# A small fp32 product behind the first round of each feed-forward loop of a decoder step

## The reference

```python
x = x + 0.5 * swiglu(rms_norm(x, p['norm_ffn1']), p['ffn1_w_gu'], p['ffn1_w_down'])
h = rms_norm(x, p['norm_mix'])
z = h @ p['w_in']
...                                   # retention, RWKV-7 recurrence
merged = (jax.nn.sigmoid(zgr) * (o_ret @ p['w_ret_o'])
          + jax.nn.sigmoid(zgw) * (o_rwkv @ p['w_rwkv_o']))
x = x + merged @ p['w_out']
x = x + 0.5 * swiglu(rms_norm(x, p['norm_ffn2']), p['ffn2_w_gu'], p['ffn2_w_down'])

def swiglu(x, w_gu, w_down):
    gate, up = jnp.split(x @ w_gu, 2, axis=-1)
    return (jax.nn.silu(gate) * up) @ w_down
```

## Time and profile before

| | |
|---|---|
| three runs | 2836.80, 2853.76, 2853.82 us |
| their median | 2853.76 us |
| profiled execution | 2833.03 us, span 2831.2 us, mean granted clock 0.997 |
| PE busy | 2803.7 us (99%), 24,662 matmul records |
| DVE busy | 1563.9 us (55%) |
| ACT busy | 1116.5 us (39%) |
| matmuls of the down loops | 3 lines x 1408 |

### The profile page before, as it was taken

How to read it: one execution, slowest core, us unless ns; L and a number is a source line. 1 busy time by engine, 2 the same in 40 slices (tenths; PEclk the granted TensorE clock), 3 DMA queues, 4 the chain that set the end, 5 groups by cost and what they waited for, 6 DMA issues and landing times.

```text
span 2831.2 us, 57289 instructions
## 1 busy us (share of the span) xinstructions
PE 2803.7 (99%) x24662; PEld 2731.8 (96%) x24662; DVE 1563.9 (55%) x1679; ACT 1116.5 (39%) x1121; POOL 107.1 (4%) x144
## 2 busy tenths in 40 slices
PE   9999999999999999999999999999999999999998
PEld 8999999999999999898998999999999999999998
DVE  6544444454566576775865655466544544444454
ACT  5333333333344453544534644233433333333333
POOL 0000000000000002011020010000000000000000
PEclk9999999999999999999999999999999999999999
DMA  5444454444556543635436544555444445444454
GB/s 209 168 169 162 165 179 171 173 168 157 172 189 235 199 174 123 235 135 201 163 134 240 188 145 164 190 201 202 164 165 176 159 164 180 170 174 164 159 173 146
DMA packets 85460, 495.80 MB, mean 175 GB/s; under 512 B 10320, under 2 KB 10496, under 8 KB 44096
## 3 DMA queue, kind: packets, MB, share of 16 engines
q1 hardware_dynamic: 71424, 444.14, 44.7%
q0 software_dynamic: 9280, 32.72, 3.2%
q10 hardware_dynamic: 4608, 16.78, 1.5%
HBM read 462.80 MB, written 30.80 MB: 174 GB/s over the span
## 4 chain that ended last, share of the span: by engine, by line
PE 89%; DVE 5%; DMA 3%; ACT 2%; issue 1%; SPq 0%; ACTq 0%; DVEq 0%; POOLq 0%
PE psum L546 28%; PE psum L547 27%; PE psum L548 27%; DVE sb_w_lo L1507 1%; DMA out_ret_s<-sb_s_ret 1%; DVE sb_w_lo L1513 1%; ACT sb_w_hi L1086 1%; PE psum L894 1%; DMA sb_raw<-in_w_wo 1%; DMA sb_s_ret<-in_s_ret 1%; PE psum L710 1%; DVE sb_s_ret L1884 0%; ACT sb_w_hi L1095 0%; DMA sb_raw<-in_gu 0%; PE psum L907 0%
## 5 line engine op out<-in xcount | busy, mean ns | idle before, releaser
L546 PE MATMUL psum<-sb_h,sb_w_hi 128*128 128x288 f32 x4384 | 1303.7, 297 | 4.6 <-DVE sb_w_lo L1507 2.2
L547 PE MATMUL psum<-sb_h,sb_w_hi 128*128 128x288 f32 x4384 | 1278.8, 292 | 0.0
L548 PE MATMUL psum<-sb_h,sb_w_lo 128*128 128x288 f32 x4384 | 1275.1, 291 | 0.0
L1513 DVE TENSOR_TENSOR sb_w_lo<-sb_raw,sb_w_hi 128x2048 fp32r<-128x2048 f32 (+1 forms) x348 | 712.3, 2047 | 697.1 <-ACT sb_w_hi L1086 696.4
L1086 ACT ACTIVATE sb_w_hi<-sb_raw 128x2048 fp32r<-128x2048 f32 (+1 forms) x349 | 600.1, 1719 | 1176.9 <-PE psum L548 1140.2
L546 PEld LDWEIGHTS psum<-sb_h,sb_w_hi 128*128 128x128 f32 x4384 | 823.5, 188 | 29.0 <-issue 19.0
L548 PEld LDWEIGHTS psum<-sb_h,sb_w_lo 128*128 128x128 f32 x4384 | 825.4, 188 | 0.0
L547 PEld LDWEIGHTS psum<-sb_h,sb_w_hi 128*128 128x128 f32 x4384 | 824.0, 188 | 1.3 <-issue 1.0
L546 PE MATMUL psum<-sb_g,sb_w_hi 128*128 128x288 f32 x1408 | 412.5, 293 | 0.0
L547 PE MATMUL psum<-sb_g,sb_w_hi 128*128 128x288 f32 x1408 | 409.7, 291 | 0.0
L548 PE MATMUL psum<-sb_g,sb_w_lo 128*128 128x288 f32 x1408 | 408.3, 290 | 0.0
(11 more groups left out here) (380 smaller groups left out, 2385.8 us busy)
## 6 DMA issues: line engine op xcount, KB each, us to landing
sb_raw<-in_gu SPq DMA_DIRECT2D x175, 1024.0 KB, 4.8
sb_raw<-in_down SPq DMA_DIRECT2D x128, 704.0 KB, 4.1
sb_raw<-in_w_mix SPq DMA_DIRECT2D x72, 1024.0 KB, 5.1
sb_raw<-in_w_gates SPq DMA_DIRECT2D x32, 1024.0 KB, 5.4
sb_s_ret<-in_s_ret POOLq DMA_DIRECT2D x32, 512.0 KB, 8.1
out_ret_s<-sb_s_ret ACTq DMA_DIRECT2D x32, 512.0 KB, 5.3
sb_raw<-in_w_ro SPq DMA_DIRECT2D x16, 1024.0 KB, 4.8
sb_raw<-in_w_out SPq DMA_DIRECT2D x16, 1024.0 KB, 4.8
```

Source lines behind the costliest of these rows:

```text
L546: pe.matmul(out, wh, xh, start=start, stop=False)
L547: pe.matmul(out, wh, xl, start=False, stop=False)
L548: return pe.matmul(out, wl, xh, start=False, stop=stop)
L1513: dve.tensor_tensor(w_lo[:, slot, 0:cols], raw[:, slot, 0:cols], w_hi[:, slot, 0:cols].bitcast(F32), ALU.subtract).then_inc(lo_made, 2)
```

## The change

A function `in_step` issues one fp32 matmul with `mean_w` both as weights and, in its first 64 columns, as moving data, into bank 7. It is called behind the second `pair` of round 0 of each up loop and each down loop, so eight times in all. The result is not read.

```diff
+STEP = 64
...
+            def in_step():
+
+                pe.matmul(psum[:, 7, 0:STEP], mean_w[:, :], mean_w[:, 0:STEP], start=True, stop=True)
+
...
                         pair(i, up_ph, 2, 1, 2, KT, h_hi, h_lo, between=mean(2 * n) if enter else None, unit=8 if n else 16)
+                        if is_first(i):
+                            in_step()
                     loop(pe, HT // 2, up)
...
                         pair(i, down_ph, 4, 1, 4, HT, g_hi, g_lo)
+                        if is_first(i):
+                            in_step()
                     loop(pe, 4, down)
```

## The result

The changed kernel is slower: 2887.86 us (median of 4 runs, 2878.59 to 2895.92), against 2845.28 us for the kernel before (median of 4 runs, the three known ones and a fourth, 2836.51 to 2853.82). The ratio is 1.0149, 95% interval 1.0096 to 1.0202. So it is slower by 1 to 2%. 2839 us and a range of 2832 to 2863 were predicted. The profiled execution took 2895.92 us.

What follows compares the result with a forecast made beforehand. The prediction took PE to be the bound, number of products times the distance between starts. The low unprofiled run of 2836.80 us plus 2.5 us for eight products, with loops at 128.9 ns, gave 2839 us, range 2832 to 2863.

Steps and rivals of the forecast that it cites:

- What bounds the kernel: Whole kernel: PE is busy 2803.7 of 2831.2 us, so time is number of products times distance between their starts.
- The own price: Added products, eight places: 0.31 us each, 2.5 us in all, with nothing hidden or credited back.
- The distance after it: Later rounds of all feed-forward loops, 10,848 products: likeliest stays at or returns to 128.9 ns, costing nothing.
- the case that I gave 0.05: Feed-forward loops: added product tips the stream into 135.4 ns, 70.5 us more, 2906.0 us, 1.8% slower; chance 0.05.
- Twice the columns: Transposes at L667: their doubled column count was given as a reason against the loops following them into 135.4 ns.
- Rival 3: Feed-forward loops: added product tips them into 135.4 ns, 70.5 us more, 2906.0 us, 1.8% slower; chance 0.05.
- Rival 1's second leg: Feed-forward loops: added product leaves the distance as it finds it and only costs 2.5 us, 2856.3 us; rival's chance 0.20.
- Rival 2: All eight feed-forward loops: tipped into 131.1 ns, 24.4 us more, 2859.9 us, up to 2863.7; chance 0.13.

Runs made afterwards that it cites:

- e1: Changed kernel with the added product called only in the four up loops, not in the down loops; 2918.06 us.
- e2: Changed kernel with the added product called only in the four down loops; 2860.10 us (median of 10 runs), ratio 1.0060.
- e3: Changed kernel with 128 moving columns in place of 64 in all eight added products; 2894.91 us (one run).
- e9: Changed kernel with the down loops' added product replaced by a single-pass one of 64 columns on h_hi; 2876.81 us (one run).
- e10: Changed kernel with the down loops' added product replaced by an fp32 one of 288 columns, moving h_hi; 2920.22 us (one run).
- e11: Changed kernel with two fp32 products of 64 columns in a row in the down loops, one in the up loops; 2876.83 us (one run).
- e13: Changed kernel measured once more with no edit; 2890.73 us (median of 4 runs), ratio 1.0170 to the kernel before.
- e7: Changed kernel with 288 moving columns, from h_hi read as fp32, in all eight added products; 2838.27 us (median of 10 runs), ratio 0.9987.
- e5: Changed kernel with the added product issued twice in a row in all eight places; 2839.32 us (median of 10 runs), ratio 0.9985.
- e12: Changed kernel with 13 single-pass 64-column h_hi products instead, early in round 0 of every feed-forward loop and the output projection; 2835.16 us (median of 12 runs).
- e8: Changed kernel with the added product inside the last group of round 0, behind high x high, instead of behind the group; 2877.53 us (one run).
- e6: Changed kernel with all eight added products single-pass, 64 columns, using h_hi as weights and moving data; 2838.84 us (one run).

## Why the prediction was wrong

*What bounds the kernel* was right: the time is products times distance, at a full clock, and 58 of the 63 us came from the distance. That a small foreign product can move it, and that the way stays until the next break, was also right: e1 shows it over some 990 groups.

*The own price* was taken as 0.31 us each from L766, within 0 to 0.49. It measured 0.23 us, 1.8 us for eight in place of 2.5. The row of 32 columns was near enough. The estimate of 0.11 us from the Trainium skill (TensorE: Matmul & The Clock Gate, Back-to-back issue gap, with the four passes) is half of what was measured.

*The distance after it* is the step that failed: "So the likeliest is the short distance, whatever came in." It was taken from how often streams came back to 128.9 ns behind other products, 17 of 21 places, and put the harm at nothing. The runs showed 135.6 ns in place of 128.9 over 2,905 groups, 58.1 us. Two things were wrong with the step.

First, the outcome is no draw. Behind a group of three, a single fp32 product of 64 or 128 columns turned 128.9 ns into 135.6 in 29 cases of 29 (after, e1, e2, e3, e9, e10, e11, e13), and 135.6 into 128.9 in 15 of 15 (after, e3, e9, e11, e13). Since a loop's product is met by a stream at 128.9 nearly always, the case that I gave 0.05 had to come. Frequencies over unlike places said nothing about a place whose way in is fixed.

Second, I weighed the wrong neighbours. Five of my 17 were single products with 288 columns. Four of them met 128.9 ns and left it; the fifth met 131.1 (1362.92 us) and left 128.9. e7 and e10 show that such a product keeps 128.9 and 135.6, so its places said nothing of 64 columns. The other places are rows of several products, and e5 and e11 show that two in a row already act otherwise than one. The trace of before has no place with one short fp32 product behind a stream at 128.9 ns.

The places of L667 are such rows too, twelve records each. "Twice the columns" was no reason to set them aside, since e3 shows that 64 and 128 behave alike; but they differ in what comes in, and that I did not look at. Ahead of the place that went back to 128.9, and ahead of one of the three that went into 135.4 (starts as in the earlier trace rows):

```profile
959.20 0.29 PE L546 MATMUL psum<-sb_h,sb_w_hi 128*128 128x288 f32 x1
...
960.36 1.04 PE L667 MATMUL psum<-sb_ident,sb_vg 128*128 128x128 f32 x8
```

```profile
1483.64 0.30 PE L546 MATMUL psum<-sb_h,sb_w_hi 128*128 128x288 f32 x1
...
1484.83 1.03 PE L667 MATMUL psum<-sb_ident,sb_vg 128*128 128x128 f32 x8
```

Three groups take 1.16 us at the first, which is the short distance, and 1.19 at the second. The other two that went into 135.4 have 1.19 ahead of them too (1133.16 to 1134.35 us, 1310.83 to 1312.02). So behind the same row of products the outcome went with what came in, four times in four, and the trace that I had showed it before any run. Nor did my count take in single-pass products: behind the two at L806 and L807 (288 columns) 128.9 ns became 131.1 in seven of eight places, the stretch from 1617 us on the earlier trace rows among them.

*The rivals.* Rival 3 named what happened, with its price for a product (6.5 ns; 6.7 measured), but took all rounds behind a product for lost, 70.5 us. It is 58.1, since the down loop's product turns the stream back, while the down loop's round 0, which I had not counted, is at the long distance: 727 groups per half in place of 904. Rival 1's second leg, that the new product leaves the way it finds, is true of 288 columns, not of 64. Rival 2 did not come: 131.1 ns was left behind the change's product in no loop. I had read the separate read ports of the Trainium skill (TensorE: Matmul & The Clock Gate, What happens when you issue a matmul) as one distance whatever came before. The loops run at 135.6 ns in e1 and at 128.9 in e5, at a full clock, so the measurement decides against that reading for this stream; that the ports are the reason is not shown.

*The spread of the runs.* I inferred that 17 us between runs sat in the distance. The runs speak for it: with products that bring the stream back, 12 runs of e12 spread over 8.6 us and 10 of e5 over 8.8, where the kernel before beside them spread over 30.3 (17 runs) and 41.5 (18 runs), and e7, whose product keeps what comes in, over 32.0 (10 runs). And four profiles (e8, e9, e11, e13) caught the pause at the start of a second half leaving 131.1 or 135.6 ns. Over a whole half of 1,056 groups that would be 21 us. What decides it at a pause was not found. No profile of a long execution of the kernel before was had, so that its long runs are such halves is inferred, not seen.

**Still open** is why. The runs show an exchange by one short two-pass product, a return by one single-pass product (from 131.1 and from 135.6) or by two two-pass ones, no change by a single long one, and other outcomes one place further on in the group. That points to the offset in time between loads of weights and reads of moving data. No run varied that offset by itself, and e6 changed the tiles together with the passes, so it is argued, not shown.

## What to carry to other kernels

Where a kernel is one long stream of equal products, count products per microsecond in each stretch before reading waits: an engine at 99% busy and a full clock can still lose 5%. Anything foreign in the stream costs its own 0.1 to 0.5 us, and may set the pace of the next hundred; judge it by the neighbour that has the same way in, not by an average over places. If the runs of an unchanged kernel spread, look for a pace that is set at a pause, and try a cheap product behind it.

## What the runs showed of the hardware

- The same matmul stream (128x288 on newly loaded 128x128 weights, operands in SBUF at the same offsets, clock at 1.00) ran at 128.9, 131.1 or 135.6 ns a product. The first and the last lasted for up to a thousand groups and more, across a loop's branch and across a change of the operands; in the feed-forward loops 131.1 was seen over 62 groups (e8).
- One fp32 product of 64 columns behind a group exchanged 128.9 and 135.6 ns in 36 cases of 36 (25 up, 11 down), and one of 128 columns in 8 of 8. Two of 64 columns in a row (12 cases, two from 135.6 and one from 131.1), or one single-pass product of 64 columns (25 cases in e6, e9 and e12, three from 135.6 and one from 131.1), ended at 128.9. One fp32 product of 288 columns kept 128.9 (8 of 8, e7) and 135.6 (4 of 4, e10), and left 128.9 the one time that it met 131.1 (L772 of before, at 1362.92 us).
- The price of a foreign product in the stream: 0.23 us for fp32 with 64 or 128 columns, which has two records.
